# A gMLP layer with its MLP on one core: two turned blocks of the first factor taken together, and what is loaded around them

## What is computed

```
hn = rms_norm(x, norm1_g)
z  = gelu(hn @ w_in)                       # 1024 x 4096
u, v = split(z, 2)                         # 2 x (1024 x 2048)
v  = layer_norm(v) * ln_g
sv = einsum('gts,bnsge->bntge', tril(w_s), v by chunks of 128) + b_s
x  = x + (u * sv) @ w_out                  # 2048 -> 1024
x  = x + square(relu(rms_norm(x, norm2_g) @ w1)) @ w2      # 1024 -> 4096 -> 1024
out = rms_norm(x, final_g)
```

## Time and profile before

| | us |
|---|---|
| median of 3 runs | 1124.3 |
| lowest and highest of them | 1124.18, 1125.67 |
| time of the profiled execution | 1126.03 |
| its span, from the first to the last instruction | 1124.2 |
| PE busy in it | 1114.8 (99%) |
| DVE busy, ACT busy, POOL busy | 785.9, 569.4, 23.5 |

### The profile page before, as it was taken

How to read it: one execution, slowest core, us unless ns; L and a number is a source line. 1 busy time by engine, 2 the same in 40 slices (tenths; PEclk the granted TensorE clock), 3 DMA queues, 4 the chain that set the end, 5 groups by cost and what they waited for, 6 DMA issues and landing times.

```text
span 1124.2 us, 13090 instructions
## 1 busy us (share of the span) xinstructions
PE 1114.8 (99%) x5088; PEld 928.2 (83%) x5088; DVE 785.9 (70%) x833; ACT 569.4 (51%) x870; POOL 23.5 (2%) x17
## 2 busy tenths in 40 slices
PE   8999999999999999999999999999999999999997
PEld 7888888888888888888888888888888888888886
DVE  4976655688779986678658547455599575677666
ACT  6774444553554334565774365454653433433456
POOL 0000000000000000000000000000000000000240
PEclk9999999999999999999999999999999999999999
DMA  8173253272865494731353635527878354343213
GB/s 294 45 210 127 94 187 113 75 244 93 316 250 221 159 358 144 217 113 38 113 187 126 211 113 183 193 108 272 293 292 305 111 226 187 113 150 113 78 73 150
DMA packets 81933, 193.80 MB, mean 172 GB/s; under 512 B 4528, under 2 KB 10704, under 8 KB 75216
## 3 DMA queue, kind: packets, MB, share of 16 engines
q1 hardware_dynamic: 81392, 192.69, 48.7%
q10 hardware_dynamic: 480, 0.28, 0.1%
HBM read 134.24 MB, written 58.72 MB: 172 GB/s over the span
## 4 chain that ended last, share of the span: by engine, by line
PE 98%; DMA 1%; ACT 0%; DVE 0%; ACTq 0%; issue 0%
PE banks L427 32%; PE banks L432 32%; PE banks L431 32%; PE banks L496 3%; PE banks L541 1%; DMA gain_rows<-in_a_ln_g_dram 1%; DVE rows L1516 0%; ACT spare L1133 0%; PE banks L503 0%; PE banks L552 0%; PE banks L523 0%; ACT rows L1325 0%; ACT o_rms L1333 0%; ACTq L922 0%; ACTq L924 0%
## 5 line engine op out<-in xcount | busy, mean ns | idle before, releaser
L984 ACT ACTIVATE pair_high<-left_and_right 128x1024 fp32r<-128x1024 f32 x168 | 177.2, 1060 | 244.4 <-PE banks L427 193.4
L1378 DVE TENSOR_TENSOR ring_low<-left_and_right,ring_high 128x512 fp32r<-128x512 f32 x224 | 152.6, 692 | 192.7 <-ACT ring_high L954 192.3
L1386 DVE TENSOR_TENSOR pair_low<-left_and_right,pair_high 128x1024 fp32r<-128x1024 f32 x168 | 204.1, 1230 | 113.9 <-ACT pair_high L984 113.9
L954 ACT ACTIVATE ring_high<-left_and_right 128x512 fp32r<-128x512 f32 x224 | 138.4, 629 | 251.2 <-PE banks L427 155.9
L427 PE MATMUL banks<-pair_high 128*128 128x512 f32 x672 | 261.9, 390 | 0.0
L432 PE MATMUL banks<-pair_high,pair_low 128*128 128x512 f32 x672 | 261.5, 389 | 0.0
L431 PE MATMUL banks<-pair_low,pair_high 128*128 128x512 f32 x672 | 261.4, 389 | 0.0
L427 PE MATMUL banks<-s_high,ring_high 128*128 128x512 f32 x384 | 149.6, 389 | 0.0
L431 PE MATMUL banks<-s_low,ring_high 128*128 128x512 f32 x384 | 149.4, 389 | 0.0
L432 PE MATMUL banks<-s_high,ring_low 128*128 128x512 f32 x384 | 149.4, 389 | 0.0
L427 PEld LDWEIGHTS banks<-pair_high 128*128 128x128 f32 x672 | 126.1, 188 | 26.6 <-DVE pair_low L1386 0.3
(11 more groups left out here) (116 smaller groups left out, 1223.5 us busy)
## 6 DMA issues: line engine op xcount, KB each, us to landing
left_and_right<-sums SPq DMA_DIRECT2D x40, 1024.0 KB, 7.1
left_and_right<-in_mlp_w_dram SPq DMA_DIRECT2D x36, 1024.0 KB, 6.5
sums<-rows SPq DMA_DIRECT2D x34, 1024.0 KB, 5.4
left_and_right<-in_a_w_in_dram SPq DMA_DIRECT2D x19, 1024.0 KB, 6.2
v_blocks<-rows SPq DMA_DIRECT2D x8, 1024.0 KB, 4.5
left_and_right<-in_a_w_out_dram SPq DMA_DIRECT2D x8, 1024.0 KB, 9.7
rows<-in_x_dram SPq DMA_DIRECT2D x7, 1024.0 KB, 8.7
spare<-v_blocks SPq DMA_DIRECT2D x6, 1024.0 KB, 6.9
```

The source lines that it names most:

```text
L954: nc.scalar.activation(ring_high[k][:, :], right_place(n, pos)[:, k, :], ACT.Copy)\
L984: nc.scalar.activation(pair_high[pair_entry(d, pos, k)][:, :, :], pair_of(d, pos, k), ACT.Copy)\
L1378: nc.vector.tensor_tensor(ring_low[k][:, :], right_place(n, pos)[:, k, :], ring_high[k][:, :].bitcast(F32), ALU.subtract).then_inc(low_don ...
L1386: nc.vector.tensor_tensor(pair_low[e][:, :, :], pair_of(d, pos, k), pair_high[e][:, :, :].bitcast(F32), ALU.subtract).then_inc(low_done, 1)
```

## The change

It has five pieces. On SP the weight block b21 is loaded before x's blocks a21 and a22 instead of after them. On PE the turn of a21 moves from behind unit 2 to behind unit 3, directly ahead of the turn of a22. On ACT two splits of b21 move ahead of the squares of x, and the other two ahead of the eviction of a22. On DVE the two first splits of b21 and the split of a12 come ahead of `s3_rows`, and the third split too. The transfer of `g2_fours` moves from ACT's queue to SP's, behind the bias, and POOL's mask waits for the last `sum_t` of single 0.

```
-                        if n == 0 and pos == 0 and k > 0:
-                            turn(0, {1: "a12", 2: "a21", 3: "a22"}[k], set_of(1))
+                        if n == 0 and pos == 0 and k == 1:
+                            turn(0, "a12", set_of(1))
+                        if n == 0 and pos == 0 and k == 3:
+                            turn(0, "a21", set_of(1))
+                            turn(0, "a22", set_of(1))
...
             load_weight(0, "b12")
+            load_weight(0, "b21")
             load_x("a21", 4, 0, NB)
             load_x("a22", 4, NB, NB)
-            load_weight(0, "b21")
             sp.wait_ge(*landed["b21", 0])
             load_weight(0, "b22")
...
+            sp.dma_start(g2_fours[:, :, :], norm2_g.rearrange("a (h p j) -> p (a h) j", h=2, j=4)).then_inc(g2_landed, 16)
...
-            act.dma_start(g2_fours[:, :, :], norm2_g.rearrange("a (h p j) -> p (a h) j", h=2, j=4)).then_inc(g2_landed, 16)
...
                     high_combo(0, "a12")
-                    square_x((0, 1, 2, 3), 0, NB)
                     split_high(0, 1, 0)
                     split_high(0, 1, 1)
-                    evict_turned(0, "a22", set_of(1))
+                    square_x((0, 1, 2, 3), 0, NB)
                     split_high(0, 1, 2)
                     split_high(0, 1, 3)
+                    evict_turned(0, "a22", set_of(1))
...
                     sum_t(0, 0)
+                    split_low(0, 1, 0)
+                    split_low(0, 1, 1)
                     low_combo(0, "a12")
+                    split_low(0, 1, 2)
                     for k in range(4):
                         s3_rows(k)
-                    split_low(0, 1, 0)
-                    split_low(0, 1, 1)
+                    split_low(0, 1, 3)
                     sum_combo(0, "s2")
-                    split_low(0, 1, 2)
-                    split_low(0, 1, 3)
...
             pool.wait_ge(ws_landed, 16)
+            pool.wait_ge(t_summed, t_sum(0, 3))
```

## The result

| us | before | changed |
|---|---|---|
| median of 20 runs each | 1124.76 | 1127.40 |
| lowest and highest | 1124.04, 1126.17 | 1125.39, 1127.66 |
| profiled execution | 1126.03 | 1125.45 |
| its span | 1124.2 | 1123.6 |

What follows compares the result with a forecast made beforehand. PE, busy for 99% of the span, was taken as the bound. From the median 1124.3, the terms -0.6 + 2.4 - 0.4 + 1.5 = +2.9 gave 1127.2, range 1125.0 to 1128.4.

Steps and rivals of the forecast that it cites:

- s3_rows behind three splits: DVE's s3_rows comes later and holds PE at a22's last bank: +2.4 us, between +1.8 and +2.6.
- The second dip: Clock falls to 1.2 GHz around or behind PE's new hole at a22's turn: +1.5 us, bounds 0 and 2.7.
- the likeliest case: Both PE holes as reckoned, clock falling at the second: 1127.2, range 1126.1 to 1128.3, chance 0.46.
- the rival "the clock stays up": Clock doesn't fall through the new hole before a22's turn: 1125.7, bounds 1124.9 to 1126.3, chance 0.32.
- The first dip: Opening: PE's shorter wait for the gains keeps the clock up: -1.5 us in executions like the profiled one, otherwise 0.
- g2_fours: Opening: off ACT's queue, the gains land sooner and the first unit begins earlier: -0.6 us, between 0 and -0.75.
- The mask: POOL's mask no longer slows DVE's splits before position 2: -0.4 us where PE runs earlier, 0 in the profiled execution.
- The loads: b21 ahead of a21 and a22 costs 0, with 1.4 and 2.3 us of cover for a21 and a22.
- My cover of 1.4 us: Margin by which a21 was to land before PE wants it, with everything running 2.1 us earlier.

Runs made afterwards that it cites:

- DVE's old order: The changed kernel with DVE again taking low_combo and s3_rows ahead of the splits of b21: 1123.97, ratio 0.9992.
- later or sooner on DVE: The changed kernel with a useless subtraction ahead of low_combo (1126.56 to 1128.81), or with s3_rows ahead of the third split (1124.71 to 1125.93).
- the kernel with g2_fours and the mask: The kernel before with g2_fours on SP's queue and the mask waiting for the last sum_t of single 0: 1123.93, ratio 0.9992.
- the four kernels of that kind without the late `s3_rows`: g2_fours moved: alone 1124.44; with the mask 1123.93; also with b11's first rows split earlier 1123.38; changed kernel with DVE's order undone 1123.97.
- only the loads: The kernel before with b21 loaded ahead of x's a21 and a22: 1125.34, ratio 1.0006.
- only the mask: The kernel before with POOL's mask waiting for the last sum_t of single 0: 1124.29, ratio 0.9996.
- turns, loads and orders: The changed kernel with g2_fours back in ACT's queue and the mask at its old place: 1126.34, ratio 1.0020.
- g2_fours alone: The kernel before with only the transfer of g2_fours issued by SP behind the bias: 1124.44, ratio 0.9997.
- the useless subtraction: The changed kernel with one needless subtraction on DVE ahead of low_combo, so that s3_rows comes later: 1126.56 to 1128.81.

## Why the prediction was right

- **s3_rows behind three splits, +2.4.** Right in place and size. Forecast was an end at 30.37 less what the opening gains; the first unit ended 14.06 - 11.37 = 2.69 sooner, and `s3_rows` at 24.95 + 2.72 = 27.67, which is 30.36 less 2.69. PE's wait, forecast at 1.7, was 1.9. Undone alone, it gave back all of the loss (DVE's old order), and later or sooner on DVE moved the end with it. In time it cost less than 2.4. Against the kernel with g2_fours and the mask, `s3_rows` ended 2.4 later counted from each profile's first product (27.67 - 8.40 and 25.47 - 8.62), but the lower cluster's middle, 1125.6, is only 1.7 above that kernel's median.
- **The second dip, +1.5.** Right: 1.54 by the chain of the profile that caught it. It comes in 12 of 20 and 4 of 11 executions, so "I expect a fall" was too flat; it is a matter of each execution. That the first 20 runs held more with the dip than without, and so gave a median next to my figure, was luck. The two medians of the same kernel, 1127.40 and 1125.93, are the forecast of the likeliest case (1127.2) and that of the rival "the clock stays up" (1125.7). Both occur.
- **The first dip, -1.5 or 0.** Right. With g2_fours off ACT's queue it was in none of 44 runs (the four kernels of that kind without the late `s3_rows`), against 22 of 91. The profiles go with the length of PE's wait for `gain_rows`: 1.8 and 1.9 us in the two with a clock of 0.50 behind it (the kernel before, only the loads), 1.0 in the two that kept 1.00 with g2_fours still on ACT's queue (only the mask; turns, loads and orders).
- **g2_fours, -0.6.** Right in sign for the profile only, where the first product came 1.1 sooner (8.40 against 9.49). I had taken the end of DVE's first low part, 8.67, for fixed, and so capped the gain; it ended at 7.57 + 0.68 = 8.25, as both its inputs came sooner. The landing was off too: PE turned the gains at 6.35 without a wait, so `gain_rows` had landed a us before the earliest time that I gave, 7.45, and no run shows what the small pieces' turns cost it. The start varies, besides, between executions of any kernel: 8.62 in the one with only the mask moved, where PE did wait for `gain_rows`. In the medians g2_fours alone gave nothing that can be told. So -0.6 was too much here as 2.4 was there; the two misses partly cancel in the sum, and that is luck as well.
- **The mask, -0.4 where the clock stays up.** 0.5 between the medians of the two kernels with g2_fours. At its new place the same slow pair of splits appears (2.18 from 72.50), under cover. The Trainium skill, "SBUF — State Buffer", section "Who interferes with whom", has the later of the two instructions wait for the earlier one's end; here the `sum_t` issued at 32.01, while POOL ran from 31.82 to 32.91, took 0.75 more, somewhat less than the 0.9 that were left of POOL's, so the trace agrees roughly.
- **The loads, 0.** Right for the changed kernel, whose waits show no transfer at a21 or a22. My cover of 1.4 us was thin: with DVE's old order PE waits 0.4 for a22, which landed at 24.60 and not at 24.0, with the useless subtraction it waits 0.3 for a21, and the new order of loads alone in the old kernel costs 0.8 by the medians, part of it by dips that I can't explain.

## What to carry to other kernels

When two transposes go through the same banks, the reader of the first is part of the second's path: count what stands ahead of that reader on its own engine before moving anything there. A small transfer in front of the first products costs more than its own length if the wait lets the clock fall; so did a hole of 1.9 us behind unit 3. Where the runs of one kernel form clusters, look at the granted clock of each run, and compare cluster with cluster: a median, or a profile, can be of either.

## What the runs showed of the hardware that I had not expected

- Behind a wait of PE of 1.9 us, with some 2 us of transposes on each side, 16 of 31 executions of one program are in the cluster of the dip (one of them profiled, at 0.50); with one of 1.0 us none of 11. Length isn't all: a profiled hole of 3.0 us kept its clock.
- The opening's pace differs between executions of kernels with the same opening, and with it the start of all work: the 8 transposes of a11 took 1.09 us in one profile and 1.97 in another, where the stretch table has the clock at 1.00 in both. The cause isn't shown.
- The 2.00 us of POOL's mask in the earlier trace rows are not the mask alone. A DVE instruction (1481) was running until 32.16, the first 1.05 of them; the mask's 1.42 in the changed kernel begin 0.46 ahead of the end of DVE's first split. Both leave about 0.95. In the profile of turns, loads and orders, where DVE stood idle beside it, the mask took 1.10:

```profile
29.01 1.10 POOL L1913 TENSOR_SCALAR_AFFINE_SELECT ws_nat<-ws_nat 128x1024 f32<-128x1024 f32 x1 [27.41 <-DMA ws_nat<-in_a_ws_dram]
```
